# Attention pipeline of the first block: value products one step later, scores ahead of the turning

## The reference, cut to what matters

```python
s = jnp.einsum('bqhcd,bkhcd->bhcqk', qb, k).astype(jnp.float32) * scale + bias[None]
pr = masked_softmax(s, mask)
a = pr[:, :, 0] - lam_full * pr[:, :, 1]
return jnp.einsum('bhqk,bkhe->bqhe', a.astype(v.dtype), v)
```

## Time and profile before

| | |
|---|---|
| timed runs | 3357.56, 3367.99, 3382.05 us; median 3367.99 |
| the profiled execution | 3352.99 us, its span 3351.2 us |
| mean granted clock of PE | 0.953 of full |
| PE busy | 3146.5 us, 94% of the span |
| DVE busy | 1944.2 us, 58% |
| ACT busy | 1527.4 us, 46% |
| chain that ended last | PE 83%, DVE 9%, ACT 6%, issue 2% |

### The profile page before, as it was taken

How to read it: one execution, slowest core, us unless ns; L and a number is a source line. 1 busy time by engine, 2 the same in 40 slices (tenths; PEclk the granted TensorE clock), 3 DMA queues, 4 the chain that set the end, 5 groups by cost and what they waited for, 6 DMA issues and landing times.

```text
span 3351.2 us, 54578 instructions
## 1 busy us (share of the span) xinstructions
PE 3146.5 (94%) x24022; PEld 3018.1 (90%) x24022; DVE 1944.2 (58%) x2298; ACT 1527.4 (46%) x2051; POOL 3.1 (0%) x8
## 2 busy tenths in 40 slices
PE   8899998899998999799999999998999999999899
PEld 8699996899978999699989987988999998898899
DVE  4555555455554555555466677555665567764564
ACT  5543454443544335543443564553434356454433
POOL 0000000000000000000000000000000000000000
PEclk9999987899999999999899999999999999999999
DMA  7245441155432554245455443433555544353453
GB/s 252 76 161 185 149 151 51 51 176 183 137 126 102 193 174 158 69 151 183 136 166 190 143 145 120 134 118 126 195 183 167 181 148 139 109 159 101 136 192 101
DMA packets 388202, 487.36 MB, mean 145 GB/s; under 512 B 33021, under 2 KB 334284, under 8 KB 387709
## 3 DMA queue, kind: packets, MB, share of 16 engines
q1 hardware_dynamic: 386828, 476.50, 43.8%
q0 software_dynamic: 848, 6.32, 0.5%
q10 hardware_dynamic: 288, 1.05, 0.1%
HBM read 480.63 MB, written 3.18 MB: 144 GB/s over the span
## 4 chain that ended last, share of the span: by engine, by line
PE 83%; DVE 9%; ACT 6%; issue 2%; DMA 0%; DVEq 0%; ACTq 0%; SPq 0%
PE ps L387 24%; PE ps L388 24%; PE ps L389 24%; DVE wl L370 3%; ACT wh L360 2%; PE ps L455 2%; DVE ar L2039 1%; PE ps L1007 1%; ACT ar L924 1%; PE ps L892 1%; PE ps L901 1%; PE ps L2188 0%; PE ps L464 0%; DVE ar L957 0%; DVE sm L962 0%
## 5 line engine op out<-in xcount | busy, mean ns | idle before, releaser
L370 DVE TENSOR_TENSOR wl<-raw,wh 128x2048 fp32r<-128x2048 f32 x456 | 1036.3, 2277 | 765.5 <-ACT wh L360 765.2
L387 PE MATMUL ps<-ah,wh 128*128 128x256 f32 x4232 | 1223.4, 289 | 30.2 <-DVE al L504 13.7
L388 PE MATMUL ps<-al,wh 128*128 128x256 f32 x4232 | 1215.0, 287 | 0.0
L389 PE MATMUL ps<-ah,wl 128*128 128x256 f32 x4232 | 1214.4, 287 | 0.0
L360 ACT ACTIVATE wh<-raw 128x2048 fp32r<-128x2048 f32 x456 | 863.6, 1899 | 627.1 <-PE ps L389 622.0
L387 PEld LDWEIGHTS ps<-ah,wh 128*128 128x128 f32 x4232 | 831.4, 196 | 35.4 <-issue 28.7
L388 PEld LDWEIGHTS ps<-al,wh 128*128 128x128 f32 x4232 | 831.7, 197 | 0.1
L389 PEld LDWEIGHTS ps<-ah,wl 128*128 128x128 f32 x4232 | 830.3, 196 | 0.0
L387 PE MATMUL ps<-ar_r,wh 128*128 128x256 f32 x2368 | 682.9, 288 | 51.2 <-DVE ar_r L2563 20.7
L388 PE MATMUL ps<-ar_r,wh 128*128 128x256 f32 x2368 | 678.8, 287 | 0.0
L389 PE MATMUL ps<-ar_r,wl 128*128 128x256 f32 x2368 | 678.5, 287 | 0.0
(11 more groups left out here) (364 smaller groups left out, 2688.6 us busy)
## 6 DMA issues: line engine op xcount, KB each, us to landing
raw<-in_ffn_w SPq DMA_DIRECT2D x264, 512.0 KB, 4.4
raw<-in_mlp_w SPq DMA_DIRECT2D x256, 512.0 KB, 4.3
raw<-in_w_in SPq DMA_DIRECT2D x124, 512.0 KB, 4.5
raw<-in_da_w_in SPq DMA_DIRECT2D x48, 512.0 KB, 4.7
raw<-in_ple_gate_w SPq DMA_DIRECT2D x32, 512.0 KB, 4.4
raw<-in_w_ssd_out SPq DMA_DIRECT2D x32, 512.0 KB, 4.3
raw<-in_fox_w_in SPq DMA_DIRECT2D x24, 512.0 KB, 4.7
raw<-in_nsa_w_in SPq DMA_DIRECT2D x20, 512.0 KB, 5.1
```

Source lines behind the costliest of these rows:

```text
L370: nc.vector.tensor_tensor(wl[:, slot, 0:sizes[n]], raw[:, slot, 0:sizes[n]], wh[:, slot, 0:sizes[n]].bitcast(F32), ALU.subtract).then_inc( ...
L387: nc.tensor.matmul(o, wa, xa, start=start, stop=False)
L388: nc.tensor.matmul(o, wa, xb, start=False, stop=False)
L389: return nc.tensor.matmul(o, wb, xa, start=False, stop=stop)
```

## The change

Three things are moved, and three buffers change.

1. On PE a turn of the loop is scores(j+2), turn(j), values(j-1); the last values stand behind the loop. turn(j) now also waits for probs(j-1) (`s_pc`), which reads the banks that it writes. The early turning of the result stands ahead of values(n-2) and waits for n-4 finished outputs in place of n-2.
2. On DVE a turn of the loop is scaled(j+2), out(j-1). scaled(j) waits for turn(j-2) (`s_pt`), since the scores no longer stand behind it.
3. On ACT square(j-2) stands where square(j-1) stood.
4. `ptb` has two buffers, `sums` four, `osq` (the squares that nobody reads) two in place of five.
5. `kwin` is gone. NSA's selected keys are stored once per group in the even chunks of `qk`, the window keys in the odd ones: 8 copies in place of 16, then 8 as before.

```diff
@@ pe_attention: turn, values, the loop
             def turn(j):
                 E.eng.wait_ge(s_e, e + j + 1)
+                if j:
+                    E.eng.wait_ge(s_pc, pc + j)
...
-                    nc.tensor.matmul(o[:, 0:wide], ptb[:, c, 0:P], value(j, c, 0), start=True, stop=True)
+                    nc.tensor.matmul(o[:, 0:wide], ptb[j % 2][:, c, 0:P], value(j, c, 0), start=True, stop=True)
...
             for j in range(n):
-                turn(j)
                 if j + 2 < n:
                     scores(j + 2)
-                elif j + 1 == n and last is not None:
+                turn(j)
+                if j + 1 == n and last is not None:
                     last(od)
-                values(j)
+                if j:
+                    values(j - 1)
+            values(n - 1)
@@ act_attention
-                probs()
-                if squares and j:
-                    square(j - 1)
+                probs(j)
+                if squares and j >= 2:
+                    square(j - 2)
             if squares:
+                square(n - 2)
                 square(n - 1)
@@ dve_attention: scaled, the loop
                 E.eng.wait_ge(s_sc, E.next(s_sc))
+                if j >= 2:
+                    E.eng.wait_ge(s_pt, pt + j - 1)
...
                 if j + 2 < n:
                     scaled(j + 2)
-                out(j)
+                if j:
+                    out(j - 1)
+            out(n - 1)
@@ pe_turn_half
-                    E.eng.wait_ge(s_od, od + n - 2)
+                    E.eng.wait_ge(s_od, od + n - 4)
@@ act_nsa
                     for half in (slice(0, 64), slice(64, P)):
-                        if v == 0:
-                            for r in range(2):
-                                last = nc.scalar.activation(qk[half, 2 * g + r, 1, :], src, ACT.Copy)
-                        else:
-                            last = nc.scalar.activation(kwin[half, g, :], src, ACT.Copy)
+                        last = nc.scalar.activation(qk[half, 2 * g + v, 1, :], src, ACT.Copy)
```

More of the change, by code:

```diff
@@ L900, in values @@
                     o = ps[:, 6 + j % 2, c * S:(c + 1) * S]
[L901 to L903 removed]
+                    nc.tensor.matmul(o[:, 0:wide], ptb[j % 2][:, c, 0:P], value(j, c, 0), start=True, stop=True)
+                    nc.tensor.matmul(o[:, P:P + wide], ptb[j % 2][:, c, P:2 * P], value(j, c, 0), start=True, stop=False)
+                    mm = nc.tensor.matmul(o[:, P:P + wide], ptb[j % 2][:, c, 2 * P:], value(j, c, 1), start=False, stop=True)
                 mm.then_inc(s_o, E.adds(s_o))
@@ L923, in exps, with probs @@
                         x = scb[:, j % 2, c, a:b]
-                        act = nc.scalar.activation(x, x, ACT.Exp, bias=nm[:, j % 2, c, q:q + 1], accum_out=sums[:, j % 3, c, q:q + 1])
+                        act = nc.scalar.activation(x, x, ACT.Exp, bias=nm[:, j % 2, c, q:q + 1], accum_out=sums[:, j % 4, c, q:q + 1])
                 act.then_inc(s_e, E.adds(s_e))
-            def probs():
+            def probs(j):
                 E.eng.wait_ge(s_pt, E.next(s_pt))
-                nc.scalar.activation(ptb[:, :, :], ps[:, 4:6, 0:384], ACT.Copy).then_inc(s_pc, E.adds(s_pc))
+                nc.scalar.activation(ptb[j % 2][:, :, :], ps[:, 4:6, 0:384], ACT.Copy).then_inc(s_pc, E.adds(s_pc))
             def square(j):
                 E.eng.wait_ge(s_od, E.next(s_od))
-                if E.seen(s_hn, 4):
-                    E.eng.wait_ge(s_hn, E.sofar(s_hn, 4))
+                if E.seen(s_hn, 1):
+                    E.eng.wait_ge(s_hn, E.sofar(s_hn, 1))
                 for q in range(NT):
-                    act = nc.scalar.activation(osq[:, j % 5, q, :], o4[:, q, j, :], ACT.Square, accum_out=hs[:, 8 * q + j:8 * q + j + 1])
+                    act = nc.scalar.activation(osq[:, j % 2, q, :], o4[:, q, j, :], ACT.Square, accum_out=hs[:, 8 * q + j:8 * q + j + 1])
                 act.then_inc(s_hn, E.adds(s_hn))
@@ L950, in dve_attention @@
         def dve_attention(E, n, kind, scale, table, wide=64):
+            pt = E.n.get(s_pt, 0)
             def scaled(j):
                 E.eng.wait_ge(s_sc, E.next(s_sc))
+                if j >= 2:
+                    E.eng.wait_ge(s_pt, pt + j - 1)
                 for a, b in COLS:
@@ L967, in out @@
                 E.eng.wait_ge(s_e, E.next(s_e))
-                nc.vector.reciprocal(r, sums[:, j % 3]).then_inc(s_d, E.adds(s_d))
+                nc.vector.reciprocal(r, sums[:, j % 4]).then_inc(s_d, E.adds(s_d))
                 E.eng.wait_ge(s_d, E.sofar(s_d))
@@ L998, in dve_attention @@
                     scaled(j + 2)
-                out(j)
+                if j:
+                    out(j - 1)
+            out(n - 1)
+            E.skip(s_pt, n)
         def pe_scores_heads(keys_of, fox=False):
@@ L1238, in build @@
         hs = view(sm, 128, [P, 16])
-        osq = view(ar, 13056, [P, 5, NT, P])
+        osq = view(ar, 13056, [P, 2, NT, P])
         def pe_da(E):
@@ L2277, in values @@
                     o = ps[:, 6, c * S:(c + 1) * S]
-                    nc.tensor.matmul(o[:, 0:P], ptb[:, c, 0:P], vm[:, 0, j, c, :], start=True, stop=True)
-                    nc.tensor.matmul(o[:, P:S], ptb[:, c, P:2 * P], vm[:, 0, j, c, :], start=True, stop=False)
-                    mm = nc.tensor.matmul(o[:, P:S], ptb[:, c, 2 * P:], vm[:, 1, j, c, :], start=False, stop=True)
+                    nc.tensor.matmul(o[:, 0:P], ptb[0][:, c, 0:P], vm[:, 0, j, c, :], start=True, stop=True)
+                    nc.tensor.matmul(o[:, P:S], ptb[0][:, c, P:2 * P], vm[:, 0, j, c, :], start=True, stop=False)
+                    mm = nc.tensor.matmul(o[:, P:S], ptb[0][:, c, 2 * P:], vm[:, 1, j, c, :], start=False, stop=True)
                 mm.then_inc(s_o, E.adds(s_o))
@@ L2380, in probs @@
                 E.eng.wait_ge(s_pt, E.next(s_pt))
-                nc.scalar.activation(ptb[:, :, :], ps[:, 4:6, 0:384], ACT.Copy).then_inc(s_pc, E.adds(s_pc))
+                nc.scalar.activation(ptb[0][:, :, :], ps[:, 4:6, 0:384], ACT.Copy).then_inc(s_pc, E.adds(s_pc))
             def turned(b):
@@ L2542, in turned @@
                 last.then_inc(s_ol, E.adds(s_ol, 2))
+            E.skip(s_pt, 4)
             scaled(0)
```

7 lines of the change are left out of this document (3 added, 4 removed).

## The result

The changed kernel takes 3349.37 us, the median of five runs (3344.17 to 3351.81). The kernel before, run beside it, takes 3373.61 (3357.56 to 3382.11). The ratio is 0.9936, 95% interval [0.9907, 0.9965]: 24 us less by the medians, 0.64% or 22 us by the ratio. The profiled executions lie closer together than the medians, 3347.5 us of span against 3351.2, and why is the subject of the experiments.

The account below looks back on a forecast made before the run. PE's weight products, 94% busy, bound the kernel; in the attentions, waits round the engines and NSA's half clock. NSA 18.4, DA 8.2 and FOX 2 sum to 28.6, so 29 us off the 3368.0 median: 3339 us, range 3320 to 3357.

Parts of the forecast that it names:

- the sum: All four attentions: NSA 18.4, DA 8.2, FOX 2, together 28.6 us; chance 0.63, ends 3324 to 3346.
- NSA's clock: NSA after its first steps: filled pauses keep PE at full clock, 14.2 steps of 3.38 us, gain 16.8 us.
- the head: Start of both DA attentions and NSA: scores(2) runs during ACT's first exponentials, 1.6 us saved in each; FOX 0.
- The step: NSA's full-clock step falls from 3.92 to DVE's unbroken 3.38 us; DA's from 3.95 to 3.67.
- DA: Each DA attention gains 1.6 us at its start, 1.7 in the middle, 0.8 at the end: 4.1, both 8.2.
- FOX: FOX attention: PE-bound step stays 6.12 us; earlier last scores and perhaps less half clock at the end gain 2 us.
- The copies: Ahead of NSA's attention: eight fewer ACT copies save half of 5.27 us, but worth 0, ends -1 to +1.
- Swings as before: Rival, chance 0.20: NSA's clock still swings, so NSA gains 6.3 us and the others 10.2; time 3351 us.
- No new round: Rival, chance 0.12: DVE still pauses each step, steps stay 3.92 and 3.95; starts and ends gain 8, 3360 us.
- half clock in all attentions: Rival, chance 0.05: denser turnings bring PE to half clock in all attentions, 29 us slower, 3397 us.
- the same gain from the median: Whole kernel: the 29 us gain, first set against the profiled 3353.0 us, is taken from the timed median 3368.0: 3339 us.
- The sign of being wrong: Behind the attention: saved time comes back where weight blocks were rounded ahead and PE can use them at once.

Follow-up runs that it names:

- the first pair: First profiled executions of the kernel before and the changed kernel, no further edit: spans 3351.2 and 3347.5 us.
- the second: Second profiles of the kernel before and the changed kernel, both rerun without further edit: medians 3375.39 and 3352.5 us.

## Why the prediction was right, and where it was not

The median of 3349.4 lies in the range, 10 us above the forecast of 3339, and within 1% of the time before. The sign and the mechanism held. That the sum came so close is in part luck, by two errors that partly cancel: the attentions gave 36 us where 28.6 were counted, and by the medians some 12 of them were taken back where nothing was counted.

- **NSA's clock**, the largest term, went as forecast behind the head. In the old order NSA has 41.0 to 41.5 us at half clock in each of five profiles and takes 80.0 to 80.7 us. In the seven with the new order the clock is 1.00 from 20.5 us behind the first scaling at the latest, the head has 0 to 17.1 us at half clock, and NSA takes 56.2 to 62.0 us. The gain is 23.6 us in the first pair and 18.6 in the second, 18.4 forecast. In the first pair the step gives 2.7 us of the difference (3.19 us where DVE's unbroken step was read as 3.38, for 14.2 steps), and the other 2.5 lie in its head and end. The Trainium skill, page "TensorE: Matmul & The Clock Gate", section "A second HAM failure mode: psum-queue depth-cycling", blames swings of the clock on small idle times between groups of matmuls, and NSA agrees. By the section "Part 4: PE-mode transpose" of the same page of the Trainium skill transposes don't count as a busy PE in the same way, and the swings might have stayed; they didn't, with a turning of 0.87 us in each step of 3.19. Whether transposes count isn't shown by that.
- **The step** was mis-sized because one row was read where others stood. In the earlier trace rows the next scaling came 0.53 us behind the start of the last operation of an output (555.31 to 555.84). After the change it is 0.35 (556.74 to 557.09), but three later steps of the trace before had that already (583.26 to 583.61 in the first of them), and a step of 3.19:

```profile
580.42 1.02 DVE L957 SCALAR_TENSOR_TENSOR ar<-ps,ar 128x256 f32<-128x256 f32 x2 [1.94 <-PE ps L1007]
...
583.61 1.01 DVE L957 SCALAR_TENSOR_TENSOR ar<-ps,ar 128x256 f32<-128x256 f32 x2
```

  DA's step is 3.52 where 3.67 was read the earlier trace rows; the last DA before the change shows 3.52 too (scalings at 1372.23 and 1375.75). The shortest step of the old trace is the one to take.
- **DA** gained 6.4 and 5.3 us, not 4.1. The steps give 0.9 of the difference. The first DA also lost its time at half clock, 6.8 us of it at its head, where the forecast had counted scores(2) alone.
- **FOX** gained 1.1 in the first pair and 2.7 in the second, 2 forecast; its turnings stand 6.12 us apart (972.98 and 979.11) as in the earlier trace rows.
- **The copies** were worth nothing, as forecast. What is left of them takes 3.1 us, 2.6 forecast.
- **The rivals.** "Swings as before" gave 3351, closer to the time than the forecast, but for a reason that is refuted: behind its head NSA didn't swing. "No new round" (3360) and "half clock in all attentions" (3397) are refuted by the same windows.
- **The step that failed** is "the same gain from the median": it took the clock outside the attentions as given, and looked for the spread of the runs in NSA. NSA's 41 us at half clock in all five profiles of the old order are no source of spread, and the profile that the sum started from was faster than any timed run. With the pause removed from both kernels, the gain of the attentions arrives, 37 us by the medians.
- **The sign of being wrong** that the prediction named, time that comes back behind NSA at once, where PE can use the rounded blocks, isn't seen. Of the 9.1 us that came back before FOX in the first pair some 8 are the fall at layer 1's perceptron (64 products of 0.12 us in the windows above), 280 us behind NSA's start.

What stays open is why the change goes with more falls at the perceptrons' ends. The count shows it, 19 of 24 ends with the change or a part of it against 3 of 8 without, but these are six profiles and two, and each part alone has them, NSA's (3 of 4) as well as DA's and FOX's (3 of 4). So I can't say that one part causes them, nor exclude that any shift of the later program does. Nor is it known why the stretch behind the last attention, the same code but for the pause, takes 1954.5 to 1957.3 us in all five profiles that have the new order in DA and the pause, and 1942.6 to 1948.9 in the other eight. With the pause gone both are gone.

## What to carry to other kernels

When a round goes over three engines, find the operation in it that stands behind another's next step and let it run one step late; the new step is then that of the engine with the most work in it, and it is read from the shortest step of the old trace in which that engine didn't wait. A gain in one stage arrives in full only if the clock in the others holds: before forecasting from one profile, look for places where TensorE pauses for a couple of microseconds, and compare the half-clock time of several runs. Of two edits, the one that removes such a pause may be worth as much as the change itself, here by the medians 24 us for the change, 29 for the pause and 65 for both (22, 17 and 58 by the ratios).

## What the runs showed of the hardware that I had not expected

- A pause of 1.9 us in an otherwise full PE was followed by 13.7 to 17.1 us at half clock in some executions and by none in others of the same kernel. With 0.4 us it was followed by at most 3.4 us, at all 20 ends of five profiles.
- A PE without pauses doesn't always get its clock back: 81.9 us busy of 81.9 in FOX at a granted clock of 0.50. In another execution it came back after 54.7 us of the same. The Trainium skill, page "TensorE: Matmul & The Clock Gate", section "Part 1: The HAM clock gate", lets the clock follow how busy PE has been, which this stretch doesn't bear out. It also warns that the records of the clock can be unreliable; here the durations agree with them, a pair of scores at 1.15 us in place of 0.63. What is not recorded is the time before the first change of the clock.
- The scatter of this kernel is mostly clock. In the first profiled pair the attentions' gain of 36.3 less 0.44 of the 71 us more at half clock elsewhere makes 5 us, and the spans differ by 3.6. A stretch at half clock costs less than half of its length here, since a weight product takes 0.213 us in place of 0.120 and not twice the time.
